# A two-block fp32 transformer kernel: stages begun tile by tile, four modulation features moved over two stage borders, heads' banks rotated

## The reference, cut to what matters

```
def first_block(x, ...):
    for l in range(2):
        h = x @ w_in[l]                      # 416 low columns, then 4608 wide ones
        ...                                  # MLA attention (8 heads), differential attention (4 heads)
        g = sigmoid(gates + b_merge[l])
        merged = g[..., :1024] * y_a + g[..., 1024:] * y_b   # y_a, y_b: products with w_branch_a, w_branch_b
        out = merged @ w_out[l]
        x = layer_norm(ALPHA * x + out, ln_gamma[l], ln_beta[l])
    return x

def second_block(x, c, ctx, c_ctx, ...):
    # mod_lat = silu(c) @ mod_w[i] + mod_b[i], 9 x 1024 values; mod_ctx the same from c_ctx
    for i in range(2):
        x = half_ffn_sublayer(x, mod_lat, 0, ...)     # starts with x * (1 + scale) + shift
        if i == 0: ctx = half_ffn_sublayer(ctx, mod_ctx, 0, ...)
        y = window_sink_attention(...) if i == 0 else fourier_mix(...)
        x = post_norm_update(x, y, mod_lat, 1, ...)
        x = half_ffn_sublayer(x, mod_lat, 2, ...)
```

## Time and profile before

| | |
|---|---|
| median of 3 runs | 1650.0 us (1645.94 to 1652.79) |
| the profiled execution | 1650.56 us, of which the span of the trace is 1648.9 us |
| PE busy | 1582.0 us (96%) |
| DVE busy | 1212.2 us (74%) |
| ACT busy | 795.4 us (48%) |
| POOL busy | 137.8 us (8%) |
| granted PE clock, mean | 0.983 |

### The profile page before, as it was taken

The page is one execution under the profiler, slowest core; times in us unless marked ns, Lnnn a source line. Parts: engine busy times, 40 slices in busy tenths (PEclk is TensorE's granted clock), DMA queues, the critical chain, the costliest instruction groups (busy, mean ns, idle before and its releaser), DMA issues.

```text
span 1648.9 us, 20705 instructions
## 1 busy us (share of the span) xinstructions
PE 1582.0 (96%) x7749; PEld 1312.0 (80%) x7749; DVE 1212.2 (74%) x1847; ACT 795.4 (48%) x1241; POOL 137.8 (8%) x205
## 2 busy tenths in 40 slices
PE   6999989999989999999999899999999999999997
PEld 5888868888778888888888568888888888888885
DVE  6888888887877775877758768877587766575544
ACT  4565535566444453444535555444354443264442
POOL 1100001100001110011100111111011110000000
PEclk9999989999999999999999999999999999999998
DMA  8865448753568876588755307887668875265551
GB/s 282 300 222 166 155 155 314 243 172 133 183 212 269 279 271 239 175 276 279 255 201 173 103 25 232 286 286 265 193 227 283 274 257 175 90 216 180 183 183 68
DMA packets 200508, 349.63 MB, mean 212 GB/s; under 512 B 11188, under 2 KB 128236, under 8 KB 199900
## 3 DMA queue, kind: packets, MB, share of 16 engines
q1 hardware_dynamic: 174668, 252.90, 46.8%
q0 software_dynamic: 25744, 95.43, 16.5%
HBM read 347.21 MB, written 1.08 MB: 211 GB/s over the span
## 4 chain that ended last, share of the span: by engine, by line
PE 84%; DVE 11%; ACT 1%; DMA 1%; issue 1%; SPq 0%; DVEq 0%; POOLq 0%
PE acc L590 24%; PE acc L592 24%; PE acc L591 24%; DVE w_lo L1503 2%; PE turn L938 1%; PE acc L844 1%; DVE gated L1928 1%; PE score L731 1%; PE score L824 1%; PE score L1024 1%; DVE acc_ctx L1624 1%; DMA mod_raw<-in_mod_w 1%; DVE att_work L2072 1%; DVE x L1604 1%; PE turn L833 1%
## 5 line engine op out<-in xcount | busy, mean ns | idle before, releaser
L1503 DVE TENSOR_TENSOR w_lo<-raw,w_hi 128x1024 fp32r<-128x1024 f32 (+2 forms) x490 | 582.4, 1195 | 268.3 <-ACT w_hi L1139 267.6
L1139 ACT ACTIVATE w_hi<-raw 128x1024 fp32r<-128x1024 f32 (+2 forms) x490 | 504.2, 1040 | 484.3 <-PE acc L592 450.3
L590 PE MATMUL acc<-w_hi,xT_hi 128*128 128x512 f32 (+1 forms) x1440 | 574.4, 399 | 8.5 <-DVE xT_lo L1539 4.5
L592 PE MATMUL acc<-w_hi,xT_lo 128*128 128x512 f32 (+1 forms) x1440 | 563.8, 392 | 0.0
L591 PE MATMUL acc<-w_lo,xT_hi 128*128 128x512 f32 (+1 forms) x1440 | 563.0, 391 | 0.0
L590 PEld LDWEIGHTS acc<-w_hi,xT_hi 128*128 128x128 f32 x1440 | 273.2, 190 | 62.9 <-issue 9.9
L592 PEld LDWEIGHTS acc<-w_hi,xT_lo 128*128 128x128 f32 x1440 | 272.6, 189 | 57.3
L591 PEld LDWEIGHTS acc<-w_lo,xT_hi 128*128 128x128 f32 x1440 | 273.4, 190 | 53.1
L488 POOL DMA_DIRECT2D mod_raw<-in_mod_w x144 | 104.3, 724 | 943.1 <-DVE mod_run L1624 758.0
L590 PE MATMUL acc<-w_hi,hT_hi 128*128 128x512 f32 x440 | 172.0, 391 | 0.1
L592 PE MATMUL acc<-w_hi,hT_lo 128*128 128x512 f32 x440 | 171.2, 389 | 0.0
(11 more groups left out here) (284 smaller groups left out, 1338.4 us busy)
## 6 DMA issues: line engine op xcount, KB each, us to landing
raw<-in_ffn_wi SPq DMA_DIRECT2D x220, 512.0 KB, 4.8
mod_raw<-in_mod_w POOLq DMA_DIRECT2D x144, 512.0 KB, 5.9
raw<-in_ffn_wo SPq DMA_DIRECT2D x110, 512.0 KB, 4.4
raw<-in_w_in SPq DMA_DIRECT2D x72, 512.0 KB, 6.4
raw<-in_w_out SPq DMA_DIRECT2D x16, 512.0 KB, 4.5
raw<-in_attn_wqkv SPq DMA_DIRECT2D x16, 512.0 KB, 4.5
wide<-in_b_merge POOLq DMA_DIRECT2D x4, 1024.0 KB, 8.6
raw<-in_w_branch_a SPq DMA_DIRECT2D x8, 512.0 KB, 4.7
```

Source lines behind the costliest of these rows:

```text
L590: nc.tensor.matmul(dst, xh, wh, start=start, stop=False)
L592: return nc.tensor.matmul(dst, xl, wh, start=False, stop=stop)
L1139: nc.scalar.activation(piece_part(w_hi[:, i % SPLIT_SLOTS, :], i), piece_part(raw[:, s, i % 2 * PIECE:(i % 2 + 1) * PIECE], i), ACT.Copy). ...
L1503: nc.vector.tensor_tensor(piece_part(w_lo[:, i % RAW_PIECES, :], i), piece_part(raw[:, i // 2 % RAW_SLOTS, i % 2 * PIECE:(i % 2 + 1) * PIE ...
```

## The change

At the two borders after a layer of the first block (layer 0 to layer 1, layer 1 to the first `ffn`) the next stage now begins tile by tile, by `project_first`. Features 4 to 7 of chunk 4 (`CHUNK_LATER = 4`) move over the border: DVE does them between the first splits of the next stage, and PE's `mod_sum` of that chunk follows the next stage's first product. In the branch stage, features 3 and 4 come before the scaled groups, feature 5 stays between the second half's splits, 6 and 7 come after the first `merge`. The groups of the heads and of the attention's pairs start with the SCORE banks (`(u + 2) % 4`); the heads no longer wait for all four banks, the attention only for TURN[0]. At the start of layer 0 the fillers ahead of tile 1 are gone.

```diff
-BRANCH_FEATURES = [(3, 4), (5, 6), (7,), ()]
+BRANCH_FEATURES = [(), (5,)]
+CHUNK_LATER = 4
 ...
 # PE, start of a layer
-                after = turn(lambda t, k: x[:, t, k * P:k * P + P], x_tile, wait=(0, 6))
-                keep_busy("acc0", 5)
-                project(ACC[0:2], 4, n=LOW, after=after)
+                if l == 0:
+                    after = turn_x()
+                    keep_busy("acc0", 5)
+                    project(ACC[0:2], 4, n=LOW, after=after)
+                else:
+                    project_first(ACC[0:2], n=LOW)
+                    mod_sum(True)
                 project(ACC[2:4], 4)
 ...
 # PE, heads
-                        b = turn_bank((first + u) % 4)
+                        b = turn_bank((first + u + 2) % 4)
 ...
-                landed(*TURN, *SCORE)
 ...
 # PE, end of a layer
                 mod_sum(True)
                 project_by_tile(ACC[2:4])
-                mod_sum(True)
 ...
 # PE, ffn
                     project_first(ACC[0:2], kept)
+                if owed:
+                    mod_sum(True)
 ...
 # PE, attention
-                landed(*TURN, *SCORE)
+                landed(TURN[0])
 ...
-            after = turn_x(wait=(0, 6))
-            keep_busy("acc0", 5)
-            after = ffn(after, True, turn_ctx_in, by_tile=False)
+            after = ffn(None, True, turn_ctx_in, by_tile=False, owed=True)
 ...
 # ACT, end of a layer
-                norm_root()
+                norm_root(then=lambda: turn_tile(mod_lat[:, 0, :], 0, 0) if l else plain_tile(0))
 ...
 # DVE, start of a layer
-                split_and_mod(8, range(8), True)
+                if l == 0:
+                    split_and_mod(8, range(8), True)
+                else:
+                    split_and_mod(4, range(CHUNK_LATER, KD), True)
+                    split_and_mod(2, range(0, 4), True)
+                    mod_store(*chunk_at(l - 1, 4))
+                    mods_stored()
+                    split_and_mod(2, range(4, 8), True)
 ...
 # DVE, branch stage
+                for k in (3, 4):
+                    mod_feature(k, True)
 ...
-                split_and_mod(1, BRANCH_FEATURES[2], True)
+                for k in (6, 7):
+                    mod_feature(k, True)
 ...
 # DVE, out product
-                split_and_mod(3, BRANCH_FEATURES[3], True)
-                split_and_mod(2, range(0, 4), True)
-                split_and_mod(1, range(4, 7), True)
+                split(4)
+                split_and_mod(2, range(CHUNK_LATER), True)
+                split()
 ...
-                mod_feature(7, True)
-                layer_norm(update, lambda t: wide[:, t, 0:D], between=split, at_root=lambda: mod_store(*ctx_chunk(4)))
-                mods_stored()
+                if l:
+                    layer_norm(update, lambda t: wide[:, t, 0:D], **by_tile)
+                else:
+                    layer_norm(update, lambda t: wide[:, t, 0:D], between=split, at_root=lambda: plain_tile(0))
 ...
 # DVE, ffn
+                if owed:
+                    chunk(0, range(CHUNK_LATER, KD), into=mod_sum_lat[:], ctx_too=True)
+                else:
+                    chunk(0, n=4 - early)
```

More of the change, by code:

```diff
@@ L924, in _, with ffn @@
                 project_by_tile(ACC[2:4])
-                mod_sum(True)
-            def ffn(after, mods, then=None, kept=False, by_tile=True):
+            def ffn(after, mods, then=None, kept=False, by_tile=True, owed=False):
                 def turn_hidden(half):
@@ L1211, in norm_root, with turn_tile, plain_tile @@
                     split(ahead - EARLY - 2)
+            def turn_tile(mod, j, t):
+                act.wait_ge(moved["score1"], c.now("score1") + 1)
+                for half in range(2):
+                    g = 2 * t + half
+                    src, place = filled(turn_bank(g)), places[(g + 2) % 4]
+                    for i in range(4):
+                        at, k = slice(i * P, i * P + P), 4 * half + i
+                        scale, shift = ((3 * j + i) * KD + k for i in (1, 0))
+                        m = nc.scalar.activation(place[:, at], src[:, at], ACT.Identity, bias=mod[:, shift:shift + 1], scale=mod[:, scale:scale + 1])
+                    m.then_inc(turn_scaled, 1)
+            def plain_tile(t):
+                for half in range(2):
+                    src = filled(turn_bank(2 * t + half))
+                    nc.scalar.activation(xT_hi[:, 4 * half:4 * half + 4, t * P:t * P + P], src[:].rearrange("p (k n) -> p k n", n=P),
+                                         ACT.Copy).then_inc(turn_hi, 1)
             split(LEAD)
             for l in range(LAYERS):
-                turn_plain(xT_hi)
+                if l == 0:
+                    turn_plain(xT_hi)
+                else:
+                    plain_tile(1)
+                    c.next("score1")
                 c.next("score1", 4)
@@ L1464, in second_tile @@
                 nc.scalar.preload_act_table(ACT.Silu)
-            nc.scalar.preload_act_table(ACT.Silu)
-            turn_modulated(mod_lat[:, 0, :], 0)
+            second_tile(0, 0)
+            c.next("score1")
             ffn(x, True, (mod_ctx, 0))
@@ L1651, in kept_store, with turn_tile, second_tile, plain_tile @@
                 mods_stored()
+            def turn_tile(t, halves=range(2)):
+                for half in halves:
+                    sl = lambda r: r[:, 4 * half:4 * half + 4, t * P:t * P + P]
+                    turn_scaled_group(2 * t + half, sl(xT_hi), sl(xT_lo), places[(2 * t + half + 2) % 4])
+            by_tile = dict(between=split, before_end=lambda: turn_tile(0, (0,)), at_root=lambda: turn_tile(0, (1,)))
+            def second_tile():
+                split()
+                turn_tile(1)
+                split(LEAD - EARLY - 2)
+            def plain_tile(t):
+                for half in range(2):
+                    b = turn_bank(2 * t + half)
+                    c.next(b)
+                    dve.wait_ge(turn_hi, c.next("hi"))
+                    sl = lambda r: r[:, 4 * half:4 * half + 4, t * P:t * P + P]
+                    nc.vector.scalar_tensor_tensor(out=sl(xT_lo), in0=bank[b][:].rearrange("p (k n) -> p k n", n=P), scalar=1.0, in1=sl(xT_hi).bitcast(F32),
+                                                   op0=ALU.mult, op1=ALU.subtract).then_inc(moved[b], 1)
+            chunk_at = lambda l, n: (0, bass.ds(l * (4 * CTX_CHUNKS) + 4 * n, 4), True)
             split(EARLY + 1)
             for l in range(LAYERS):
-                turn_plain(xT_hi, xT_lo, splits=True)
+                if l == 0:
+                    turn_plain(xT_hi, xT_lo, splits=True)
+                else:
+                    split()
+                    plain_tile(1)
+                    split(LEAD - EARLY - 2)
                 for i, src in enumerate((cols[:, bass.ds(2 * l + G_Q, 1)], cols[:, bass.ds(2 * l + G_Q + 1, 1)],
@@ L1962, in acc_uses, with ffn, chunk @@
                     c.next(b + " moved", first if i < 2 else last)
-            def ffn(x, ready, mod, j, mods=None, rows=32, then=False, end={}, early=0):
-                def chunk(half, features=(), n=4, into=None):
+            def ffn(x, ready, mod, j, mods=None, rows=32, then=False, end={}, early=0, owed=False):
+                def chunk(half, features=(), n=4, into=None, ctx_too=False):
                     for i in range(n):
```

55 lines of the change are left out of this document (21 added, 34 removed).

## The result

The changed kernel takes 1653.4 us (median of 20 runs, 1647.8 to 1655.0), the kernel before 1649.6 us (20 runs, 1645.0 to 1652.8). The ratio is 1.0026, 95% interval 1.0018 to 1.0034: slower by 3.8 us (3.0 to 5.6). That is inside the predicted range (1636 to 1655), but the forecast was 4.35 us faster, and the sign is wrong.

The account below looks back on a forecast made before the run. The prediction took PE, busy 96%, as the bound. Border of layer 0 3.05, border of layer 1 2.5, heads -1.6 and attention 0.4 gave 4.35 us off 1650.56: 1646.2 us, range 1636 to 1655.

Parts of the forecast that it names:

- the branch stage: Features moved into DVE's idle time and behind the first merge: out product starts 3.7 us sooner.
- the full clock behind it: Out products keep full clock, 1.0 us back in layer 0, 2.2 in layer 1; their ends 4.4 and 5.6 sooner.
- both moved sums: Sums of chunk 4 behind the borders: PE idles 6.4 and about 7.4 us there for DVE's features.
- the rotation: New order of SCORE banks at the heads: second group starts 0.8 us later in each layer.
- the attention: First maximum no longer waits for scores behind `landed`: 0.4 us gained (0 to 0.55).
- The start of layer 0: Fillers gone there cost and give nothing; not priced.
- The step "heads": Heads of both layers: a loss of 0.8 us in each, 1.6 together.
- border of layer 0: Layer 0 to layer 1: 1.3 us lost of 4.4, net 3.05 gained; products and loads queue behind PE's wait.
- Rival B: Modulation weights of chunk 0 come late in layer 1; kernel slower than before, 1663.1 or 1654.6 us; chance 0.10.
- The term "clock 2.0": Lower clock behind PE's wait at each of the two borders: 2.0 us each (bounds 1.0 and 2.6).
- B in full: Late weights in both following chunks of layer 1: 12.5 us slower, 1663.1 us; chance given as 0.05.

Follow-up runs that it names:

- e2: The changed kernel with the six fillers ahead of tile 1 at the start of layer 0 back as before; 1653.2 us, ratio 1.0026.
- e9: The changed kernel with 28 and 30 fillers on PE ahead of the sum of chunk 4 at the two borders; 1645.9 us, ratio 0.9991.
- e3: The changed kernel with the heads' order of banks and wait for all four banks as before, attention still rotated; 1651.3 us, ratio 1.0012.
- e6: The changed kernel with POOL's loads of the merge bias and norm rows behind those of chunk 1; 1649.7 us, ratio 1.0006.
- e8: The changed kernel with the edits of e1, e2 and e3 together and the merge bias loaded behind chunk 1; 1633.6 us, ratio 0.9908.
- e12: The changed kernel with the edits of e1, e2 and e3 and the merge bias loaded behind the latents' chunk; 1635.6 us, ratio 0.9919.
- e1: The changed kernel with the sum of chunk 4 one product later at both borders; 1635.7 us, ratio 0.9922.
- e11: The changed kernel with the sum of chunk 4 one product later at the border of layer 1 alone, not the ffn's; 1646.1 us, ratio 0.9993.
- e5: The changed kernel with 54 and 60 fillers on PE ahead of the sum of chunk 4 at the two borders; 1658.5 us, ratio 1.0057.
- e4: The kernel before with only the branch stage's features placed anew; 1642.8 us, ratio 0.9963.

## Why the prediction was wrong

What held: the 3.7 us of the branch stage, the full clock behind it (4.5 and 5.7 by the table, for 4.4 and 5.6), that both moved sums would meet unfinished features, and by how much (6.07 and 6.72 us for 6.4 and 7.4), the rotation's 0.8 to 1 us a layer, the attention's 0.5. The start of layer 0 was put at nothing, because the first product waits for its weights and DVE's rests anyway. It cost 0.9 us against the trace of before and 2.6 against e2's, since without the fillers the product began at half rate; e2 also shows that nothing of it reaches the end.

What failed, in the order of size:

- The step "heads", a loss of 0.8 us in each layer. In layer 1 it was 5.1. The bank's 0.8 to 1.0 is in it; 2.00 us are PE's wait for q, and about 1.7 the half rate behind it (three double groups from 330.37 to 334.65, 4.28 us for the 2.61 that they take before). What stands behind this is a sentence of the border of layer 0: what queues behind the wait "costs nothing as long as PE stands". The sentence names SP's loads alone; what it left out did cost. PE frees no slots while it stands, DVE stands 5.25 us behind it, and the load of chunk 0 that waits for DVE's features, with the bias and chunk 1 queued behind it, is 2.8 to 3.8 us late.

  Rival B has modulation weights that come late, at a chance of 0.10, but with another cause and another victim. Its loads behind features 5 and 7 were issued at 248.95 and 253.86, near the times it names, and hurt nothing (DVE waited 0.18 us for the first); the third was not later than before (257.38 for 257.82). And it tied the loss to chunk 0's own sum, which was not late (279.69 for 280.05 before). The victim was the q of the heads, 45 us behind DVE's wait for chunk 1. The earlier trace rows had the sign of it: DVE's 3.40 us for a DMA. I took it for a bound on one pair's time and did not ask whether the engines were full there. They were, in the kernel before too (columns as in the earlier trace rows, DMA share 1.03):

```profile
270.00:290.00 20.00, 20.00 (x97) 16.83 (x97) 14.96 (x31) 11.26 (x20) 2.12 (x3) 1.00 1.03 384
```

- The term "clock 2.0" behind each stall. It was 2.8 and 3.9 us by e9, so 2.7 too little; the upper bound of 2.6 was too low as well. I read it from borders at which PE waited twice for some 2 us. The remark that short gaps don't cost the clock held for 1.42 us in 9, the row it was read from, but not in general: one wait of 1.99 us at layer 1's heads in e3 was followed by 0.50 from 330 to 332 us.

4.35 us faster, less 4.3 at the heads of layer 1 and 2.7 of clock, is 2.7 us slower; 3.8 was measured, and the table has 2.8. The last us is not settled: among it is how low the clock falls behind one and the same wait, 0.80 in one execution and 0.65 in another (e6) in the window from 255 to 265. Two slips of the prediction's sums don't matter for this: 4.4 less 1.3 is 3.1 and not 3.05, and B in full has 0.04 and not 0.05.

What stays open: whether the gain of a shorter border in layer 1 can be had in full with these weights. e8 and e12 only move the wait. Loads spread over a longer time (a third slot for modulation weights) weren't tried. That DVE's 5.25 us behind the standing PE are what made the bias late is read from who waits for whom, and no run tests it by itself; in e1, where PE doesn't stand, this wait is gone and the bias is issued at 263.85, as early as before, but DVE still waits 6.87 us for chunk 1's first weights.

## What to carry to other kernels

A step moved over a border must be checked against the engine that feeds it: count what stands on that engine between the border and the step, and put the step where the count ends; one product later was worth 17.7 us here. A wait of the busiest engine is not free for the others: whoever fills its buffers stops with it. When a gain is placed ahead of a stretch in which the DMA engines are full, ask of each us whether it survives that stretch: of 11 us won, 5 did (e11), and of 2.6 none (e2). And where loads wait for buffers that the moved work frees, follow everything queued behind those loads on their queue to its first user, however far.

## What the runs showed of the hardware

A filler matmul of 128 columns took 0.22 us, as two rows of 0.11: 54 of them ran 12.2 us (e5). Waits of 6.07 and 6.72 us cost another 2.8 and 3.9 us of clock, and filling them with matmuls that nobody reads kept the granted clock at 1.00 without touching the wait itself (e9). Much shorter waits brought the clock down as well: after one of 1.75 us, with PE fully busy ahead of it, it was 0.66 in the next 2 us and 0.50 from 236 to 238 us (e4). Where the DMA share was 1.03, the core moved 384 to 396 GB/s, and the time from the issue of chunk 1's first load to its first use was 12.8 and 13.0 us in the two kernels.
